# Another order of the three products of a split fp32 matmul, and other start offsets of the activation tiles, in a two-block transformer kernel

## The reference

```python
def first_block(x, mem, ...):
    proj = rmsnorm(x, norm_mix_g) @ w_in                      # 1024 -> 3592
    h = x + concat([fox_attention(...), hgrn2(...)]) @ w_out
    h = h + cross_attention(rmsnorm(h, norm_x_g) @ w_xq, rmsnorm(mem, g) @ w_xkv) @ w_xo
    h = h + square(relu(rmsnorm(h, norm_ff_g) @ w1)) @ w2     # 1024 -> 4096 -> 1024
    return rmsnorm(h, final_norm_g)

def second_block(x, mem_2, ...):
    proj = rms_norm(x, norm_mix_pre) @ w_in_2                 # 1024 -> 7168
    mix = g0 * (diff_attention(...) @ w_attn) + g1 * (pool(...) @ w_pool) + g2 * (mem_attention(...) @ w_mem)
    x = x + rms_norm(mix @ w_out, norm_mix_post)
    up = causal_conv(rms_norm(x, norm_ffn_pre) @ w_up)        # 1024 -> 2 * 2816
    return x + rms_norm((gelu(g) * v) @ w_down, norm_ffn_post)
```

## Time and profile before

| | us |
|---|---|
| median of 3 runs | 936.27 |
| lowest and highest run | 935.83, 941.43 |
| the profiled execution, its own time | 935.83 |
| its span, first to last instruction | 934.1 |
| TensorE busy | 909.6 |
| VectorE busy | 580.4 |
| ScalarE busy | 496.8 |
| GpSimd busy | 98.6 |

### The profile page before, as it was taken

One profiled execution on the slowest core, in us unless ns is written; L12 is line 12 of the kernel. 1 busy time (PEld: TensorE's weight loads), 2 busy tenths in 40 slices (PEclk: granted clock), 3 DMA queues, 4 the chain that ended last, 5 costly groups with the idle time before them and its releaser, 6 DMA issues.

```text
span 934.1 us, 16025 instructions
## 1 busy us (share of the span) xinstructions
PE 909.6 (97%) x6412; PEld 839.4 (90%) x6412; DVE 580.4 (62%) x762; ACT 496.8 (53%) x725; POOL 98.6 (11%) x148
## 2 busy tenths in 40 slices
PE   6999999999999999999989999999999999999997
PEld 6998998887987999988879988999999899999885
DVE  4674576654644766644455438867587588888643
ACT  5774645534654655533364446766544476666531
POOL 7202122300001000000040006001000200000000
PEclk9999999999999999999999999999999999999999
DMA  8866523225442666555536554454456466775631
GB/s 254 266 226 190 180 91 134 93 91 180 139 133 91 203 190 211 184 188 209 188 102 225 182 180 136 136 181 158 143 180 203 128 182 181 201 200 182 223 137 45
DMA packets 134802, 157.52 MB, mean 169 GB/s; under 512 B 3751, under 2 KB 113565, under 8 KB 134749
## 3 DMA queue, kind: packets, MB, share of 16 engines
q1 hardware_dynamic: 133085, 151.78, 50.8%
q0 software_dynamic: 1056, 3.93, 1.1%
q10 hardware_dynamic: 608, 1.06, 0.3%
HBM read 155.71 MB, written 1.05 MB: 168 GB/s over the span
## 4 chain that ended last, share of the span: by engine, by line
PE 89%; DVE 4%; ACT 3%; issue 1%; POOL 1%; DMA 1%; SPq 0%; DVEq 0%; POOLq 0%; ACTq 0%
PE tb L567 17%; PE tb L569 16%; PE tb L568 16%; PE acc L567 10%; PE acc L568 10%; PE acc L569 10%; PE tb L645 2%; PE acc L750 1%; DMA raw<-in_w_in 1%; ACT junk L1089 1%; DVE wlo L1485 1%; ACT whi L1062 1%; DVE xlo L1498 0%; PE tb L842 0%; PE acc L973 0%
## 5 line engine op out<-in xcount | busy, mean ns | idle before, releaser
L1485 DVE TENSOR_TENSOR wlo<-raw,whi 128x2048 fp32r<-128x2048 f32 (+1 forms) x143 | 326.8, 2289 | 238.4 <-ACT whi L1062 238.3
L567 PE MATMUL tb<-xhi,wlo 128*128 128x256 f32 x1256 | 351.1, 280 | 0.9 <-DVE xlo L1498 0.6
L568 PE MATMUL tb<-xhi,whi 128*128 128x256 f32 x1256 | 348.6, 278 | 0.0
L569 PE MATMUL tb<-xlo,whi 128*128 128x256 f32 x1256 | 348.5, 277 | 0.0
L1062 ACT ACTIVATE whi<-raw 128x2048 fp32r<-128x2048 f32 (+1 forms) x143 | 272.4, 1911 | 133.5 <-PE acc L569 111.7
L567 PEld LDWEIGHTS tb<-xhi,wlo 128*128 128x128 f32 x1256 | 235.9, 188 | 2.2 <-issue 1.7
L569 PEld LDWEIGHTS tb<-xlo,whi 128*128 128x128 f32 x1256 | 236.8, 189 | 0.0
L568 PEld LDWEIGHTS tb<-xhi,whi 128*128 128x128 f32 x1256 | 236.3, 188 | 0.1
L465 POOL TENSOR_SCALAR rs<-ss 128x1 f32<-128x1 f32 x16 | 7.7, 480 | 408.2 <-ACT junk L1089 407.9
L569 PE MATMUL acc<-wlo,hid_hi 128*128 128x512 f32 x128 | 49.8, 389 | 0.0
L568 PE MATMUL acc<-whi,hid_hi 128*128 128x512 f32 x128 | 49.8, 389 | 0.0
(11 more groups left out here) (330 smaller groups left out, 1403.9 us busy)
## 6 DMA issues: line engine op xcount, KB each, us to landing
raw<-in_w_in SPq DMA_DIRECT2D x42, 1024.0 KB, 5.2
raw<-in_w SPq DMA_DIRECT2D x32, 1024.0 KB, 5.2
raw<-in_w_up SPq DMA_DIRECT2D x44, 512.0 KB, 4.9
raw<-in_w_down SPq DMA_DIRECT2D x22, 512.0 KB, 4.1
raw<-in_w_xkv SPq DMA_DIRECT2D x8, 1024.0 KB, 5.3
raw<-in_w_out SPq DMA_DIRECT2D x8, 1024.0 KB, 5.0
raw<-in_w_mem_kv SPq DMA_DIRECT2D x4, 1024.0 KB, 5.0
raw<-in_w_xq SPq DMA_DIRECT2D x4, 1024.0 KB, 5.0
```

The lines of the kernel that those rows point to most:

```text
L567: pe.matmul(o, a_lo, b_hi, start=start, stop=False)
L568: pe.matmul(o, a_hi, b_hi, start=False, stop=False)
L569: return pe.matmul(o, a_hi, b_lo, start=False, stop=stop)
L1485: dve.tensor_tensor(wlo[:, n % RING, :m], raw[:, n % RING, :m], whi[:, n % RING, :m].bitcast(F32), ALU.subtract).then_inc(lo_ready, 1)
```

## The change

The rooms of the activations get 32 spare words in place of 64, and their tiles start at word 12 in place of 48 ("rec" stays at 0). The filler `gap` has 8 words in place of 40 and `gap_m` has 16 in place of 48, and a new filler `gap_l` of 16 words stands behind `mlo`. In `mm3` the order of the three matmuls becomes high by high, high by low, low by high; it was low by high, high by high, high by low (the first named is the stationary part).

```diff
-        xhi_room = sb("xhi", [P, KT * T + 64], F32R)
-        xlo_room = sb("xlo", [P, KT * T + 64], F32R)
+        xhi_room = sb("xhi", [P, KT * T + 32], F32R)
+        xlo_room = sb("xlo", [P, KT * T + 32], F32R)
...
-        sb("gap", [P, 40])
+        sb("gap", [P, 8])
...
-                sb("gap_m", [P, 48], at=r1)
+                sb("gap_m", [P, 16], at=r1)
                 mhi = sb("mhi", [P, KT, T], F32R, at=r1)
                 mlo = sb("mlo", [P, KT, T], F32R, at=r1)
+                sb("gap_l", [P, 16], at=r1)
...
-        START = {"x": 48, "rec": 0, "h1": 48, "h2": 48, "x2": 48, "a": 48, "h4": 48}
+        START = {"x": 12, "rec": 0, "h1": 12, "h2": 12, "x2": 12, "a": 12, "h4": 12}
...
-                pe.matmul(o, a_lo, b_hi, start=start, stop=False)
-                pe.matmul(o, a_hi, b_hi, start=False, stop=False)
-                return pe.matmul(o, a_hi, b_lo, start=False, stop=stop)
+                pe.matmul(o, a_hi, b_hi, start=start, stop=False)
+                pe.matmul(o, a_hi, b_lo, start=False, stop=False)
+                return pe.matmul(o, a_lo, b_hi, start=False, stop=stop)
```

## The result

| | before | changed |
|---|---|---|
| median | 936.13 us (4 runs) | 950.28 us (4 runs) |
| lowest and highest | 935.83, 941.43 | 948.41, 951.83 |
| the profiled execution, its own time | 935.83 | 949.76 |
| its span | 934.1 | 948.0 |

The ratio, taken over all runs, is 1.0137, with a 95% interval of 1.0095 to 1.0178: slower by 1.4%, some 13 us (the two medians alone give 1.5%, 14.2 us).

The account below looks back on a forecast made before the run. The prediction took TensorE's matmul pace as the bound: order 0 us, redrawn t_slab paces +2.3 us, row slabs left as they are, 935.8 + 2.3 = 938.1 us, given as 938.5 us against the median of the runs; range 929 to 950.

Parts of the forecast that it names:

- What bounds the kernel: TensorE, busy 97% of the span: a changed matmul pace is paid in full, changes only to other engines are hidden.
- The order costs nothing: In `mm3`, the new order keeps three matmuls and three loads and moves only the seam between blocks: 0 us of itself.
- Two paces, drawn anew at each restart: In the t_slabs (256 moving columns), 0.340 or 0.353 us a triple, drawn after each break; 0.213 us a slab between them.
- the third rival: Neither seam nor offset matters; paces come from the instants at which streams restart, which are unchanged: 936.3 us, chance 0.12.
- The 512-column slabs do go by address: Slabs with stationary tile at 192 bytes are slow, 0.688 us a triple, those at 0 fast, 0.680; 0.06 us a slab.
- The likeliest case: The paces are redrawn at the new offsets: +2.3 us, 938.5 us, chance 0.45.
- I keep the draw and its odds, 13 in 31, and apply them to all: Slow odds applied to all 88.5 t_slabs: 37 slow, 10.6 more than now, +2.3 us.
- the one from above: Upper bound: every x t_slab slow, 11.9 us, plus 2.1 us if 128 is slow for 35 row slabs, 14.0 us.
- The pace there is bounded by the two that rows show: No stage had run at 48, 64, 128 or 176 bytes, so the two known paces were taken as limits there.
- 48 is a bad start: Start off a multiple of 64 bytes holds every x t_slab slow: 948.2 us, or 950.3 with row slabs; chance 0.20.

Follow-up runs that it names:

- experiment 1: The kernel before with only the three products of `mm3` in the new order, every tile where it was: median 939.82 us over 10 runs, ratio 1.0008.
- experiment 2: The changed kernel with the three products back in the old order, all tiles at their new offsets: 952.11 us over 4 runs, ratio 1.0148.
- experiments 5 to 8: The kernel before with every x tile at word 0, 16, 32 or 56 of its room: 954.93, 945.47, 950.43 and 951.62 us, two runs each.
- start56: The kernel before with every x tile at word 56 (224 bytes): 951.62 us, two runs.
- experiment 4: The kernel before with the fillers alone changed (`chi`, `hid`, `y`, `v` at 128 bytes, `phi`, `ohi` at 64): 944.59 us over 10 runs, ratio 1.0088.
- experiments 5 and 7: The kernel before with every x tile at word 0 (0 bytes) or at word 32 (128 bytes): 954.93 and 950.43 us, two runs each.
- mixed_b: The kernel before with a start per x stage, in bytes: x 208, h1 240, h2 176, x2 160, a 32, h4 96: 951.87 us, one run.
- mixed_a: The kernel before with a start per x stage, in bytes: x 80, h1 96, h2 144, x2 208, a 176, h4 160: 953.2 us, one run.
- start16: The kernel before with every x tile at word 16 (64 bytes): 945.47 us, two runs.

## Why the prediction was right or wrong

**What bounds the kernel: right.** The pace of `mm3` is paid in full: 13.4 us more busy time of TensorE, 13.9 us more span, no new wait for a slab, no other engine's busy time moved by more than 1.0 us.

**The order costs nothing: right,** shown within 0.4% by experiment 1 (ratio 1.0008) and, from the other side, by experiment 2.

**Two paces, drawn anew at each restart: right for the kernel before,** and the third rival ("the very slabs that were slow are slow again") is wrong: with every address as before, w1 and cv of experiment 1 were slow. There the order had changed; mb shows the same with its tile and the order kept, since the kernels of experiments 5 to 8 move the x tiles alone. This is mb in the profile before and in start56 (L568 with `ohi`):

```profile
L568 PE MATMUL tb<-ohi,whi x30: 276/276/276, 683.9 to 693.7; 128*128 128x256 f32 x30
...
L568 PE MATMUL tb<-ohi,whi x32: 281/281/281, 692.7 to 703.7; 128*128 128x256 f32 x32
```

The draw may well be the spread of the kernel before too, 932.4 to 945.6 us over the 36 runs beside these kernels, of which w1 and cv together could make 8.1; this is argued, since only one execution of that kernel was profiled. (The prediction counted 13 slow among 31 restarts; slab by slab over the whole trace I find 14 among 32, which would have added 0.3 us.)

**"The 512-column slabs do go by address": right in part.** At 0 bytes w2 held 0.680 in every profile that has it there. At 192 bytes there are two paces, 0.688 in the earlier trace rows, and 0.700 in vd of experiment 1 and in fv to gg of experiment 4. One profile had happened to show only one of them.

**The likeliest case, 938.5 us: wrong.** The step of the prediction that failed is "I keep the draw and its odds, 13 in 31, and apply them to all". The offsets do not shift odds, they make a set of paces of their own: 0.347 and 0.353 at 48 and 176 bytes, with no 0.340 to draw. With 0.340 gone, the two blocks that carried the fast pace, 38 slabs, could only lose.

**The bounds: the one from above was no bound.** "The pace there is bounded by the two that rows show" took 0.688 for the worst of the row slabs; 128 bytes gave 0.697, that is 35 × 8 × 0.017 = 4.8 us where I had 2.1. For the t_slabs it took 0.353; other offsets reach 0.360. It held for the changed kernel only because its x tiles happened to stay at 0.353 and below.

**The rival "48 is a bad start" came out in time and sign,** 948.2 or, with the row slabs, 950.3 us against 950.28 measured, but by two errors that cancel: the t_slabs cost some 8 us and not its 11.9, since cv, qd and kd got 0.347, and the row slabs more than its 2.1. That the sum fits is luck. Its reason, a row that begins off a multiple of 64 bytes, fell with experiments 5 and 7. I gave it 0.20, and slower by over 1% 0.22; the upper end of the range, 950.0, lies 0.3 us under the median, and it reached that far only because of this rival. The view that should have moved the chance was in my hands: the earlier trace rows show every slab at 192 bytes slower than those at 0, so that an address matters, and the earlier trace rows that 192 was a place where the fast pace exists. An offset with the fast pace was the exception to be explained, and I treated it as what any offset would have.

**The rule of the Trainium skill.** That the moving operand and the weight load use read ports of their own and never wait ("TensorE: Matmul & The Clock Gate", Part 2; "SBUF — State Buffer", Who interferes with whom) would leave all these kernels equal. The runs do not agree: with the instructions, the clock and the waits alike, a tile's offset alone moves a triple between 0.340 and 0.360 us. Nor do the other engines' accesses look like the cause: in the changed kernel each of the 16 slabs of w1 has the same 0.3533 us a triple, while VectorE's split takes 2.3 us and ScalarE's 1.9 us of the 5.6 us of a slab. "SBUF — State Buffer" (Door 1, the note on cachelines) also gives a line of 16 bytes. That 196 and 200 bytes (0.360) are slower than 192 would fit a rule about such lines, but 0, 128 and 176 are multiples of 16 as well, and are slow (0.360, 0.356 and 0.358).

## What to carry to other kernels

Where TensorE is the bound, read the distance between starts of one line's matmuls stage by stage, not the share of busy time: a few nanoseconds a matmul, with no wait to show for them, were 1.4% here. Fillers and start offsets that look idle can carry that pace, so move the SBUF layout only with this view at hand, and check every tile behind a changed filler, as a stationary tile and as a moving one. An offset that has not run has no bound from those that have; and a kernel whose runs differ by 1% may hold blocks that draw their pace, so compare its profiles block by block and its times over many runs.

## What the runs showed of the hardware that I had not expected

The pace of fp32r triples with 256 moving columns, by the byte offset of the moving tiles from the weight ring modulo 256, both tiles alike unless two are named (microseconds a triple; two values where the stream drew either):

| offset | triple | offset | triple |
|---|---|---|---|
| 0 | 0.360 | 184, 188 | 0.360 |
| 32 | 0.350 | 192 | 0.340, 0.353 |
| 64 | 0.340, 0.353 | 196, 200 | 0.360 |
| 80, 96 | 0.360 | 208 | 0.350, 0.358 |
| 128 | 0.356 | 224 | 0.355 |
| 144 | 0.350 | 240 | 0.351 |
| 160 | 0.352, 0.356 | 48 and 176 | 0.347, 0.353 |
| 176 | 0.358 | 192 and 64 | 0.353 |

The offset of 32 bytes has one block of four slabs behind it (ab in mixed_b), 240 the four of xq, 144 one of sixteen; the 0.350 at 208 is a single slab, the first of up in mixed_a, and one slab at 160 was at 0.360. Where one pace is given, another might be drawn in other runs. The ring was never moved, so the runs cannot tell the distance to it from the address itself.

With 512 moving columns, by the offset of the stationary tile: 0 gives 0.680, 128 gives 0.697, 48 with 176 gives 0.690, 0 with 128 gives 0.693, and 192 gives 0.688 or 0.700; 64 and 224 gave 0.700 too, in fv to gg of start16 and start56. The 0.700 at 192 is in fv to gg of experiment 4 and in vd of experiment 1 (L567, high by high):

```profile
L567 PE MATMUL acc<-whi,xhi x31: 397/397/398, 536.7 to 557.7; 128*128 128x512 f32 x31
```

Of all layouts tried, that of the kernel before is the fastest, and none that holds the fast pace for certain was found. Still open: what in the chip makes the paces, what at a restart decides between two of them, and whether the fast pace needs the low and the high tile at the same offset everywhere.
